# A stream-encoder step on one core: the attention's v made first, its filler moved to the loop's end, the norms' squares summed on 32-column tiles

## The chip, the cores and the metric

The kernel runs on 1 core of one Trainium2 chip. The metric is the device time of one execution in microseconds (us), lower is better. Three timed executions of the kernel before gave 3475.59, 3475.68 and 3482.91 us, median 3475.68 us.

TensorE (PE in the rows) does matmuls and transposes, VectorE is DVE, ScalarE is ACT, GpSimd is POOL, SyncE (SP) only issues DMAs. Each takes its instructions in program order and waits at semaphores. PEld rows are TensorE's weight loads.

## The reference, cut to what matters

One encoder layer over 1152 frames (1024 of a prompt and 8 running streams of 16 frames), width 1024:

```python
x = x + 0.5 * swiglu_ffn(x, ffn1_norm, ...)
h = rmsnorm(x, mix_norm); proj = h @ w_in
#   mixer A: chunk-band softmax attention, 8 heads x 64   mixer B: gated DeltaNet, 4 heads x 128
x = x + (sigmoid(gA) * (yA @ w_branch_a) + sigmoid(gB) * (yB @ w_branch_b)) @ w_mix_out
x = x + cross_attention(rmsnorm(x), K/V of 256 memory tokens)
x = x + 0.5 * swiglu_ffn(x, ffn2_norm, ...)
y = rmsnorm(x, final_norm)          # rmsnorm: x * rsqrt(mean(x*x) + eps) * g, in float32
```

Everything is float32. The memory tokens have a norm of their own before their K and V are made.

## The kernel before, in words

Activations lie transposed: 8 chunks of 128 features on the partitions, 1152 frames along the free axis, worked on in three thirds of 384 frames. A dense product of one weight unit (128 output features) with one third is `product` (L149): every float32 operand is split into a high and a low part, and 3 x 8 matmuls of 384 columns (high x high, weight high x x low, weight low x x high) add into one PSUM bank. POOL makes the split weights (`w_hi` L124 or L143, `w_lo` L127 or L146) in three slots; SP loads them.

The stages run in this order: `memory` (K and V of the memory tokens, with the first norm done beside it), `ffn1`, `attention` (mixer A), `delta` (mixer B), `merge`, `mix`, `cross`, `wo`, `ffn2`, `last`. Engines meet only by semaphores within a stage.

**The norms** (class `Norm`). For each third n: ACT squares the 8 chunks in two instructions of 4 chunks (`square`, L470); `sums` (L479) on PE multiplies each chunk of squares by a 128x128 matrix of ones, 8 float32 matmuls that add into bank 4+n, so that each partition holds the sum over all features; `root` on ACT (Ln L489, Exp L492) makes the inverse root in `n_rinv`; DVE scales the chunks into `n_tmp` (L509, 8 instructions); ACT rounds them to the high part (`upper`, L519, two instructions), DVE makes the low part (`lower`, L526). There are five norms of x with three thirds each, 15 calls of `sums`, and one call for the memory tokens (256 columns). In `ffn_phase` (both FFNs) the last turn does thirds 0 and 1 of the next norm between its own products: `sums` after the fifth down product of a third, with DVE's scaling woven among its additions. In `residual_phase` (`mix`, `wo`) `sums` follows a product of the order table; ACT then does square, root, upper of third 0 and of third 1 in a row. Third 2 is done in the stage that follows. In `memory` lists by job number (`pe_norm`, `act_norm`) say after which job each step goes; ACT there also rounds weights (L2063), copies K and V out (`m_kv`, `m_nat`) and issues their DMAs, all in one order.

**Attention** works pair by pair of heads, four pairs: pair 0 written out, pairs 1 to 3 as a hardware loop. A pair has 9 dense jobs (q, k, v by three thirds), PE taking them in that order in the loop, and by thirds in pair 0; ACT copies each from PSUM (`take`, L1021; two banks in turn, so that a job waits for the copy of the job two before). Then v is turned: 8 transposes of v (L940), 8 of the streams' v (L943), which ACT copies to `a_vn` (L1036) and `a_vns` (L1039) before the first scores (L831) may start. Nine steps follow: PE computes scores, DVE adds the bias and takes the maximum, ACT exponentiates, DVE normalises, PE turns the probabilities (L876), ACT copies them, PE multiplies them with v (`values`, L901; L888 for the streams). Step 4 is the streams' step: its scores (L838, L844) and values run on 32-column tiles, and step 5 turns the streams' output back (L909). So that PE has work meanwhile, the 12 jobs of mixer B's projections (288 matmuls, L249) are dealt out by a list, the `filler`: two places in each step, before and between the two turns of probabilities, and one place before the last values. Job 20, the last filler job, and job 0 of the next pair use the same PSUM bank; job 0 therefore waits for job 20's copy.

Of the kernel before, what the change touches and what calls it, by code (L numbers as in the profile page):

```python
# [14 lines left out]
D = 1024  # L15
# [56 lines left out]
def load_units(sp, k, first, turns, turn, at_turn=None, then=None):  # L72
# [3 lines left out]
    def one(i, j):  # L76
# [3 lines left out]
        sp.dma_start(k.w_raw[slot(j, turn)][:, :], k.units[turn * i + (first + j)])\  # L80
# [15 lines left out]
    for j in range(k.ahead):  # L96
        users = sharing(j, turn) or [turn - 1]
        sp.wait_ge(k.unit_split.sem, k.unit_split.at(turn * (turns - 1) + users[-1] + 1))
        sp.dma_start(k.w_raw[j][:, :], k.units[first + turns * turn + j]).then_inc(k.raw_landed[j].sem, 16)
# [50 lines left out]
def product(pe, out, tiles, n0, n1):  # L150

    last = len(tiles) - 1
    for part in range(3):
        for i, (wh, wl, xh, xl) in enumerate(tiles):
# [107 lines left out]
def ffn_phase(nc, k, name, norm, x, xh, xl, work, tail, bias_rows=None, memory=None):  # L262
# [24 lines left out]
    def tensor(pe):  # L287
        def turn(i):
            order = order_of(i)
            for g, (u, n) in enumerate(order):  # L290
# [17 lines left out]
                mm = product(pe, k.ps[g % NPS][:, 0:THIRD], tiles, n * THIRD, (n + 1) * THIRD)  # L308
# [7 lines left out]
            for n in range(3):  # L316
                pe.wait_ge(k.h_ready.sem, k.h_ready.at(6 * i + (3 + n + 1)))
                for d in range(KD):
# [11 lines left out]
                    if isinstance(i, int) and i == LAST and n >= 1 and d == 4:  # L330
                        tail.sums(pe, n - 1)

# [7 lines left out]
    def scalar(act):  # L340
# [18 lines left out]
        if norm:  # L359
            norm.square(act, 2)  # L360
            norm.root(act, 2)
# [74 lines left out]
class NormSignals:  # L436
# [3 lines left out]
    def __init__(self, k, name):  # L440
        self.nsq, self.ntotal = k.counter(name + "_squared"), k.counter(name + "_total")
        self.nln, self.nrinv = k.counter(name + "_ln"), k.counter(name + "_rinv")
# [5 lines left out]
class Norm:  # L448
# [24 lines left out]
    def sums(self, pe, n):  # L473

        k, s = self.k, self.s
        for c in range(KD):
            if c % 4 == 0:
                pe.wait_ge(s.nsq.sem, s.nsq.at(2 * n + c // 4 + 1))
            mm = pe.matmul(k.ps[4 + n][:, 0:self.width], k.ones[:, :], self.squares[:, c, self.cols(n)],  # L479
                           start=(c == 0), stop=(c == KD - 1))  # L480
        mm.then_inc(s.ntotal.sem, 1)

    def root(self, act, n):
        k, s = self.k, self.s
        act.wait_ge(s.ntotal.sem, s.ntotal.at(n + 1))
        if n >= 2:
            act.wait_ge(s.nscaled.sem, s.nscaled.at(2 * (n - 1)))
        r = self.rinv[:, n % 2, :]
        act.activation(r, k.ps[4 + n][:, 0:self.width], ACT.Ln, bias=k.eps[:, 0:1], scale=1.0 / D)\  # L489
# [41 lines left out]
    def tensor(self, pe):  # L531
        for n in range(self.nb):
            self.sums(pe, n)

# [8 lines left out]
    def scalar(self, act):  # L543
# [3 lines left out]
        for n in range(self.nb):  # L547
            self.root(act, n)
# [28 lines left out]
def last_norm_phase(nc, k, norm):  # L577
# [11 lines left out]
    def tensor(pe):  # L589
        norm.sums(pe, 2)  # L590

    def scalar(act):
        act.wait_ge(k.x_added.sem, k.x_added.at(NPS))
        norm.square(act, 2)
        norm.root(act, 2)
# [10 lines left out]
class Core:  # L606
# [116 lines left out]

    def counter(self, name, tokens=0):
# [36 lines left out]
def attention_phase(nc, k, norm, decay, xh, xl, x, x_to, work):  # L761
# [31 lines left out]
    filler = Filler(3, 4, [14, 8, 18, 8, 20, 8, 22, 8] + [26, 8] * 5 + [12])  # L793
# [32 lines left out]
    def tensor(pe):  # L826
# [85 lines left out]
        def job(i, g, u, n):  # L912
# [1872 lines left out]
```

## Time and profile before

| | us |
|---|---|
| median of 3 timed executions | 3475.68 |
| the profiled execution, its own time | 3480.32 |
| its span, first to last instruction | 3478.5 |
| PE busy in it | 3293.7 |
| DVE busy | 1288.3 |
| POOL busy | 954.7 |
| ACT busy | 674.7 |

The profile follows one execution of 3480.32 us. The span leaves out 1.8 us at its ends. In the span the mean granted TensorE clock was 0.983 of full speed. The matmul rows give the pipelined duration of each, with an end that is modelled; the cost of a matmul in a row of many is the distance between starts. A float32 matmul that isn't split has two records.

### The profile page before, as it was taken

How to read it: one execution, taken by the hardware profiler on the slowest of the kernel's cores; microseconds unless marked ns; L12 is line 12 of the kernel's file. 1: busy time of each engine (PE TensorE's matmuls, PEld its weight loads, DVE VectorE, ACT ScalarE, POOL GpSimd, SP SyncE). 2: the span in 40 equal slices, each digit the busy share in tenths (PEclk: the TensorE clock that was granted, in tenths of full speed). 3: DMA queues.
4: the chain of work that ended last, by engine and by line, in shares of the span. 5: the costliest groups of instructions: out<-in, count | busy, mean ns of one | idle time of the engine just before them, and what ended most of it. 6: DMA issues, size and time to landing. Idle time of an engine off the chain costs nothing. (4 is left out here: it accounts for less than half of the span.)

```text
span 3478.5 us, 50346 instructions
## 1 busy us (share of the span) xinstructions
PE 3293.7 (95%) x19945; PEld 3129.6 (90%) x19945; DVE 1288.3 (37%) x2289; ACT 674.7 (19%) x1302; POOL 954.7 (27%) x436
## 2 busy tenths in 40 slices
PE   6999999999999999988988979999799999999998
PEld 5999999999889888877887879988599999999997
DVE  3232333332445545642442454232225323233324
ACT  5100000000132422433333332123311000000001
POOL 3433333333313123101001023221123333333331
PEclk9999999999999999989999999999899999999999
DMA  5411111111232133112112144024401111111111
GB/s 181 141 37 48 42 42 42 42 36 43 83 109 107 77 119 117 60 69 80 71 38 93 45 157 156 21 96 156 147 31 43 43 48 40 42 40 41 36 48 55
DMA packets 96556, 254.24 MB, mean 73 GB/s; under 512 B 11552, under 2 KB 52640, under 8 KB 93728
## 3 DMA queue, kind: packets, MB, share of 16 engines
q1 hardware_dynamic: 45568, 146.95, 12.3%
q10 hardware_dynamic: 50848, 105.25, 8.4%
q8 instruction: 109, 1.79, 0.2%
q14 instruction: 31, 0.25, 0.0%
HBM read 199.83 MB, written 52.33 MB: 72 GB/s over the span
## 5 line engine op out<-in xcount | busy, mean ns | idle before, releaser
L124 POOL TENSOR_TENSOR w_hi<-w_raw,zero 128x1024 fp32r<-128x1024 f32 x201 | 385.4, 1917 | 2231.3 <-PE psum L155 1320.0
L155 PE MATMUL psum<-x_hi,w_hi 128*128 128x384 f32 x3024 | 598.2, 338 | 51.5 <-DVE x_lo L2136 32.2
L155 PE MATMUL psum<-x_lo,w_hi 128*128 128x384 f32 x3024 | 592.4, 335 | 0.0
L155 PE MATMUL psum<-x_hi,w_lo 128*128 128x384 f32 x3024 | 589.5, 334 | 0.0
L155 PEld LDWEIGHTS psum<-x_hi,w_hi 128*128 128x128 f32 x3024 | 533.6, 189 | 58.1 <-issue 47.6
L155 PEld LDWEIGHTS psum<-x_lo,w_hi 128*128 128x128 f32 x3024 | 533.9, 189 | 0.0
L155 PEld LDWEIGHTS psum<-x_hi,w_lo 128*128 128x128 f32 x3024 | 530.8, 188 | 0.0
L127 POOL TENSOR_TENSOR w_lo<-w_raw,w_hi 128x1024 fp32r<-128x1024 f32 x201 | 500.0, 2488 | 15.8
L394 DVE TENSOR_TENSOR f_hid<-psum,f_gate 128x384 f32<-128x384 f32 x132 | 73.6, 558 | 861.8 <-PE psum L155 859.3
L349 ACT ACTIVATE f_gate<-psum 128x384 f32<-128x384 f32 x132 | 64.7, 493 | 1477.4 <-PE psum L155 1477.4
L155 PE MATMUL psum<-f_h_hi,w_hi 128*128 128x384 f32 x1056 | 269.1, 335 | 0.0
L155 PE MATMUL psum<-f_h_hi,w_lo 128*128 128x384 f32 x1056 | 267.9, 334 | 0.0
L155 PE MATMUL psum<-f_h_lo,w_hi 128*128 128x384 f32 x1056 | 267.9, 334 | 0.0
L249 PE MATMUL psum<-x_hi,w_hi 128*128 128x384 f32 x912 | 197.1, 346 | 3.2 <-issue 2.6
L249 PE MATMUL psum<-x_hi,w_lo 128*128 128x384 f32 x912 | 199.5, 346 | 0.0
L249 PE MATMUL psum<-x_lo,w_hi 128*128 128x384 f32 x912 | 197.8, 346 | 0.0
L155 PEld LDWEIGHTS psum<-f_h_hi,w_hi 128*128 128x128 f32 x1056 | 190.7, 188 | 1.1
L155 PEld LDWEIGHTS psum<-f_h_hi,w_lo 128*128 128x128 f32 x1056 | 190.7, 188 | 0.0
L155 PEld LDWEIGHTS psum<-f_h_lo,w_hi 128*128 128x128 f32 x1056 | 190.7, 188 | 0.0
L406 DVE SCALAR_TENSOR_TENSOR x_late<-psum,x_late 128x384 f32<-128x384 f32 x264 | 145.2, 556 | 116.6 <-PE psum L155 116.6
L406 DVE SCALAR_TENSOR_TENSOR x_early<-psum,x_early 128x384 f32<-128x384 f32 x264 | 145.1, 556 | 112.7 <-PE psum L155 112.7
L249 PEld LDWEIGHTS psum<-x_hi,w_hi 128*128 128x128 f32 x912 | 157.4, 188 | 10.0 <-issue 6.9
(276 smaller groups left out, 3354.2 us busy)
## 6 DMA issues: line engine op xcount, KB each, us to landing
w_raw<-units SPq DMA_DIRECT2D x224, 512.0 KB, 3.5
gate_dram<-b_stash ACTq DMA_DIRECT2D x48, 192.0 KB, 1.9
e_gate<-gate_dram ACTq DMA_DIRECT2D x48, 192.0 KB, 2.5
a_kc<-k_cache ACTq DMA_DIRECT2D x4, 2048.0 KB, 7.5
a_vc<-v_cache ACTq DMA_DIRECT2D x4, 2048.0 KB, 13.9
x_sk<-mem_k ACTq DMA_DIRECT2D x8, 1024.0 KB, 8.5
proj_dram<-a_cv ACTq DMA_DIRECT2D x12, 576.0 KB, 2.8
b_pad<-proj_dram SPq DMA_DIRECT2D x12, 576.0 KB, 4.8
```

The source lines that it names most:

```text
L124: pool.tensor_tensor(k.w_hi[s][:, :], k.w_raw[s][:, :], k.zero[:, 0:1].to_broadcast([P, D]), ALU.add)\
L127: pool.tensor_tensor(k.w_lo[s][:, :], k.w_raw[s][:, :], k.w_hi[s][:, :].bitcast(F32), ALU.subtract).then_inc(k.unit_split.sem, 1)
L155: mm = pe.matmul(out, wl if part == 2 else wh, (xl if part == 1 else xh)[:, n0:n1], start=(part == 0 and i == 0), stop=(part == 2 and i == ...
L249: mm = pe.matmul(k.ps[g % 2][:, 0:THIRD], w[:, c * P:(c + 1) * P], (xl if part == 1 else xh)[:, c, n * THIRD:(n + 1) * THIRD], start=(r == 0),
L349: act.activation(gate[:, n, :], k.ps[g % NPS][:, 0:THIRD], ACT.Silu)\
L394: dve.tensor_tensor(hid[:, j % 2, :], up, gate[:, n, :], ALU.mult).then_inc(k.hid_made.sem, 1)
L406: dve.scalar_tensor_tensor(out=xs, in0=k.ps[g % NPS][:, 0:THIRD], scalar=0.5, in1=xs, op0=ALU.mult, op1=ALU.add).then_inc(k.x_added.sem, 1)
```

## The change

Three things are changed.

1. `Norm.sums`: the chunk c goes to column tile c % 4 (stationary operand 128x32 ones, output on 32 partitions at 32 * (c % 4)); chunks 0 to 3 start the four accumulations, chunks 4 to 7 end them. Bank 4+n then holds four partial sums, each on 32 partitions. A new `gather` on ACT copies them to `n_rinv`, and a new `total` on PE (one float32 matmul of 384 columns with the full ones) adds over all 128 partitions; every value is counted 32 times, and the Ln's scale becomes 1/(32 * D). `total` is placed one step behind `sums`: inside the next product, behind its first 8 of 24 matmuls (`between`), in the FFNs' last turn after the next down product, in `memory` two jobs later, and at once in the last norm and in the memory tokens' norm.
2. Attention: the units of a pair are loaded and made in the order v, q, k. In the loop v is turned (`turn_v`) after the sixth job, and ACT copies it (`copy_v`) after its sixth take; in pair 0 `turn_v` comes after all nine jobs. The pair's first scores wait for seven copies, step 3 for all nine.
3. The filler's list: step 4, and steps 6 to 8, give 23 instead of 26 matmuls at their first place, step 5 30; the place before the last values gives 6 instead of 12, and a new place behind the last values 14.

```diff
+def product(pe, out, tiles, n0, n1, between=None):
     for part in range(3):
+        if part == 1 and between:
+            between()
...
-            mm = pe.matmul(k.ps[4 + n][:, 0:self.width], k.ones[:, :], self.squares[:, c, self.cols(n)],
-                           start=(c == 0), stop=(c == KD - 1))
-        mm.then_inc(s.ntotal.sem, 1)
+            r = 32 * (c % 4)
+            mm = pe.matmul(k.ps[4 + n][r:r + 32, 0:self.width], k.ones[:, 0:32], self.squares[:, c, self.cols(n)],
+                           start=(c < 4), stop=(c >= 4), tile_position=(0, r))
+        mm.then_inc(s.nparts.sem, 1)
+    def total(self, pe, n):
+        pe.wait_ge(s.ngathered.sem, s.ngathered.at(n + 1))
+        pe.matmul(k.ps[4 + n][:, 0:self.width], k.ones[:, :], self.rinv[:, n % 2, :], start=True, stop=True)\
+            .then_inc(s.ntotal.sem, 1)
+    def gather(self, act, n):
+        act.wait_ge(s.nparts.sem, s.nparts.at(n + 1))
+        if n >= 2:
+            act.wait_ge(s.nscaled.sem, s.nscaled.at(2 * (n - 1)))
+        act.activation(self.rinv[:, n % 2, :], k.ps[4 + n][:, 0:self.width], ACT.Copy).then_inc(s.ngathered.sem, 1)
...
+    def nth_unit(self, phase, j):
+        return (2, 0, 1)[j] if phase == 2 and j < 3 else j
-    filler = Filler(3, 4, [14, 8, 18, 8, 20, 8, 22, 8] + [26, 8] * 5 + [12])
+    filler = Filler(3, 4, [14, 8, 18, 8, 20, 8, 22, 8] + [23, 8] + [30, 8] + [23, 8] * 3 + [6, 14])
...
         def pair(i):
-            pe.wait_ge(k.evacuated.sem, k.evacuated.at(DONE * i + (9 + ND)))
...                                         # the 16 transposes go to turn_v(i)
+            pe.wait_ge(k.evacuated.sem, k.evacuated.at(DONE * i + (7 + ND)))
             pe.wait_ge(k.vn_ready.sem, k.vn_ready.at(2 * i + 2))
             for s in range(STEPS):
+                if s == 3:
+                    pe.wait_ge(k.evacuated.sem, k.evacuated.at(DONE * i + (9 + ND)))
...
             filler.products(k, pe, i, 2 * STEPS, xh, xl)
             values(i, STEPS - 1)
+            filler.products(k, pe, i, 2 * STEPS + 1, xh, xl)
...
         with pe.Fori(1, PAIRS) as i:
             for g in range(9):
                 job(i, g, g // 3, g % 3)
+                if g == 5:
+                    turn_v(i)
...
                 take(i, g, g // 3, g % 3)
                 if g == 5:
+                    copy_v(i)
                     load_caches(i)
...
             for g in filler.finished(2 * STEPS):
                 evacuate(i, g)
             copy_o(STEPS - 1)
+            for g in filler.finished(2 * STEPS + 1):
+                evacuate(i, g)
```

Three places where PE's order shows it. First, PE in the last turn of ffn1, around the first `sums`; of before (`f_h` is the FFN's hidden vector):

```order
L155 MATMUL psum<-f_h_hi,w_lo_62 128x384
L479 MATMUL psum<-n_squares,ones 128x384 x8
L155 MATMUL psum<-f_h_hi,w_hi_58 128x384
L155 MATMUL psum<-f_h_hi,w_hi_59 128x384
L155 MATMUL psum<-f_h_lo,w_hi_58 128x384
```

and of the changed kernel:

```order
L157 MATMUL psum<-f_h_hi,w_lo_62 128x384
L489 MATMUL psum<-n_squares,ones 32x384 x8
L157 MATMUL psum<-f_h_hi,w_hi_58 128x384
L157 MATMUL psum<-f_h_hi,w_hi_59 128x384
L157 MATMUL psum<-f_h_lo,w_hi_58 128x384
L157 MATMUL psum<-f_h_lo,w_hi_59 128x384
L157 MATMUL psum<-f_h_hi,w_lo_61 128x384
L157 MATMUL psum<-f_h_hi,w_lo_62 128x384
L497 MATMUL psum<-n_rinv,ones 128x384
```

The eight full matmuls became eight of 32 output rows, and one full matmul follows a product (six matmuls) later. Second, PE in the loop from the last job to the first scores of a pair, before:

```order
L155 MATMUL psum<-x_lo,w_hi_59 128x384 x8
L155 MATMUL psum<-x_hi,w_lo_62 128x384 x8
L938 REGISTER_ALU
L940 MATMUL psum<-ident,a_v 128x128 x8
L943 MATMUL psum<-ident,a_v 16x128 x8
L945 ISA
L831 MATMUL psum<-a_k,a_q 128x128 x2
```

and now:

```order
L157 MATMUL psum<-x_lo,w_hi_59 128x384 x8
L157 MATMUL psum<-x_hi,w_lo_62 128x384 x8
L947 REGISTER_ALU
L157 MATMUL psum<-x_hi,w_hi_59 128x384 x8
L157 MATMUL psum<-x_lo,w_hi_59 128x384 x8
L157 MATMUL psum<-x_hi,w_lo_62 128x384 x8
L980 ISA
L862 MATMUL psum<-a_k,a_q 128x128 x2
```

The transposes stand three jobs earlier and nothing is between the last job and the scores. Third, PE at the end of the loop's body, before:

```order
L876 MATMUL psum<-ident,a_sc 128x128 x5
L249 MATMUL psum<-x_lo,w_hi_58 128x384 x4
L249 MATMUL psum<-x_hi,w_lo_61 128x384 x8
L882 REGISTER_ALU
L897 REGISTER_ALU
L901 MATMUL psum<-a_pt,a_vn 64x128 x10
L962 REGISTER_ALU
L962 COMPARE_AND_BRANCH
```

and now:

```order
L907 MATMUL psum<-ident,a_sc 128x128 x5
L251 MATMUL psum<-x_hi,w_hi_58 128x384 x4
L251 MATMUL psum<-x_lo,w_hi_58 128x384 x2
L913 REGISTER_ALU
L928 REGISTER_ALU
L932 MATMUL psum<-a_pt,a_vn 64x128 x10
L251 MATMUL psum<-x_lo,w_hi_58 128x384 x6
L251 MATMUL psum<-x_hi,w_lo_61 128x384 x8
L1001 REGISTER_ALU
L1001 COMPARE_AND_BRANCH
```

Six matmuls stand before the last values where 12 stood, and 14 between them and the branch.

## Rows read from the trace of the kernel before

**Rows 1.** The page's first part: busy us (share) xinstructions

```profile
PE 3293.7 (95%) x19945; PEld 3129.6 (90%) x19945; DVE 1288.3 (37%) x2289; ACT 674.7 (19%) x1302; POOL 954.7 (27%) x436
```

**Rows 2.** Groups by shape: names, shapes, xcount | busy us, mean ns | idle before

```profile
L479 PE MATMUL psum<-n_squares,ones 128*128 128x384 f32 x240 | 80.1, 487 | 3.1 <-ACT n_squares L470 3.1
L2370 PE MATMUL psum<-x_sk,x_qz 128*32 128x256 f32 x128 | 18.4, 382 | 0.0
```

**Rows 3.** The chain that ended last, stage wo: start, us, what

```profile
2602.85 5.16 PE psum L479 x16
...
2612.26 1.99 POOL w_hi L143
```

**Rows 4.** Timeline of PE, streams' step: start, us, engine, line, names, [idle before]

```profile
1164.98 1.06 PE L838 MATMUL psum<-a_kc,a_qbd 128*32 128x512 f32 x8
1165.87 0.23 PE L844 MATMUL psum<-a_k,a_qbd 128*32 128x16 f32 x8
```

**Rows 5.** Timeline: one float32 matmul of 384 columns; ACT's copy of 384 columns

```profile
1627.85 0.81 PE L1655 MATMUL psum<-b_sq,ones 128*128 128x384 f32 x2
...
982.73 0.49 ACT L1021 ACTIVATE a_q<-psum 128x384 f32<-128x384 f32 x1 [7.84 <-PE psum L155]
```

**Rows 6.** Timeline of ACT, stage mix, the squares of third 1

```profile
2242.54 2.86 ACT L470 ACTIVATE n_squares<-x_late 128x1536 f32<-128x1536 f32 x2 [2.78 <-DVE x_late L2306]
```

**Rows 7.** Timeline of PE, first turn of ffn2, the third 2

```profile
2641.67 1.63 PE L155 MATMUL psum<-x_hi,w_hi 128*128 128x384 f32 x8 [0.78 <-DVE x_lo L526]
```

**Rows 8.** Timeline of ACT and PE, end of ffn1

```profile
937.55 1.49 ACT L519 ACTIVATE x_hi<-n_tmp 128x1536 fp32r<-128x1536 f32 x1 [1.49 <-DVE n_tmp L509]
...
949.30 2.72 PE L155 MATMUL psum<-x_hi,b_w8h 128*8 128x384 f32 x8 [4.62 <-DVE b_w8l L1373]
```

**Rows 9.** Timeline of the end of the kernel

```profile
3459.90 2.86 ACT L470 ACTIVATE n_squares<-x_late 128x1536 f32<-128x1536 f32 x2 [2.58 <-DVE x_late L406]
3461.44 5.43 PE L479 MATMUL psum<-n_squares,ones 128*128 128x384 f32 x16 [2.17 <-ACT n_squares L470]
3466.90 0.58 ACT L489 ACTIVATE n_rinv<-psum,eps 128x384 f32<-128x384 f32 x1 [4.14 <-PE psum L479]
```

**Rows 10.** Timeline of stage memory, ACT and PE

```profile
15.71 0.47 ACT L489 ACTIVATE nm_rinv<-psum,eps 128x256 f32<-128x256 f32 x1 [4.52 <-PE psum L479]
...
86.89 2.08 PE L155 MATMUL psum<-mem_hi,w_hi 128*128 128x256 f32 x8 [2.37 <-POOL w_lo L2029]
```

**Rows 11.** Timeline of PE, last matmuls of pair 1's jobs to its first scores

```profile
1133.61 1.55 PE L155 MATMUL psum<-x_hi,w_lo 128*128 128x384 f32 x8
1135.74 1.09 PE L940 MATMUL psum<-ident,a_v 128*128 128x128 f32 x8 [0.58 <-ACT a_v L1021]
...
1138.84 0.49 PE L831 MATMUL psum<-a_k,a_q 64*128 64x128 f32 x4 [1.13 <-ACT a_vns L1039]
```

**Rows 12.** Timeline of pair 0's start, DVE and PE

```profile
1012.84 0.11 DVE L1168 MEMSET a_bias<- 64x64 f32 x1 [2.10 <-DMA a_bias_s<-bias_dram]
...
1017.02 0.33 PE L876 MATMUL psum<-ident,a_sc 128*128 128x128 f32 x1 [1.26 <-DVE a_sc L1198]
```

**Rows 13.** Timeline of PE at the loop's turn, pair 1 to 2 and 2 to 3

```profile
1220.99 1.31 PE L901 MATMUL psum<-a_pt,a_vn 128*64 128x128 f32 x20
1225.33 2.87 PE L155 MATMUL psum<-x_hi,w_hi 128*128 128x384 f32 x8 [3.02 <-issue]
1227.99 1.94 PE L155 MATMUL psum<-x_lo,w_hi 128*128 128x384 f32 x8
...
1354.63 2.53 PE L155 MATMUL psum<-x_hi,w_hi 128*128 128x384 f32 x8 [2.89 <-issue]
```

**Rows 14.** Busy time by window, PE alone: window, us, PE busy, granted clock, DMA share, GB/s

```profile
1225.00:1229.00 4.00, 3.67 (x12) 0.57 0.88 268
```

**Rows 15.** Timeline of PE from pair 0 into the loop

```profile
1097.42 1.68 PE L155 MATMUL psum<-x_hi,w_hi 128*128 128x384 f32 x8
```

**Rows 16.** Timeline of PE, pair 1, step 5

```profile
1185.09 0.77 PE L876 MATMUL psum<-ident,a_sc 128*128 128x128 f32 x5 [0.89 <-DVE a_sc L1198]
```

More of the change, by code:

```diff
@@ L79, in one @@
             sp.wait_ge(k.unit_split.sem, k.unit_split.at(turn * i + (last + 1 - turn * back)))
-        sp.dma_start(k.w_raw[slot(j, turn)][:, :], k.units[turn * i + (first + j)])\
+        sp.dma_start(k.w_raw[slot(j, turn)][:, :], k.units[turn * i + (first + k.nth_unit(k.phase, j))])\
             .then_inc(k.raw_landed[slot(j, turn)].sem, 16)
@@ L98, in load_units @@
         sp.wait_ge(k.unit_split.sem, k.unit_split.at(turn * (turns - 1) + users[-1] + 1))
-        sp.dma_start(k.w_raw[j][:, :], k.units[first + turns * turn + j]).then_inc(k.raw_landed[j].sem, 16)
+        sp.dma_start(k.w_raw[j][:, :], k.units[first + turns * turn + k.nth_unit(k.phase + 1, j)]).then_inc(k.raw_landed[j].sem, 16)
 def units_ahead(k):
@@ L307, in turn @@
                           xh[:, c, :], xl[:, c, :]) for c in range(KD)]
-                mm = product(pe, k.ps[g % NPS][:, 0:THIRD], tiles, n * THIRD, (n + 1) * THIRD)
+                mm = product(pe, k.ps[g % NPS][:, 0:THIRD], tiles, n * THIRD, (n + 1) * THIRD,
+                             (lambda: norm.total(pe, 2)) if order is by_third and g == 2 else None)
                 mm.then_inc(k.dense_done.sem, 1)
@@ L331, in turn @@
                         tail.sums(pe, n - 1)
+                    if isinstance(i, int) and i == LAST and n >= 1 and d == 5:
+                        tail.total(pe, n - 1)
         if memory:
@@ L360, in scalar @@
             norm.square(act, 2)
+            norm.gather(act, 2)
             norm.root(act, 2)
@@ L375, in scalar @@
         tail.square(act, 0)
+        tail.gather(act, 0)
         tail.root(act, 0)
@@ L380, in scalar @@
             tail.upper(act, 0)
+        tail.gather(act, 1)
         tail.root(act, 1)
@@ L590, in tensor @@
         norm.sums(pe, 2)
+        norm.total(pe, 2)
     def scalar(act):
@@ L594, in scalar @@
         norm.square(act, 2)
+        norm.gather(act, 2)
         norm.root(act, 2)
@@ L910, in turn_streams, with job @@
             mm.then_inc(k.ys_turned.sem, 1)
-        def job(i, g, u, n):
+        def job(i, g, u, n, between=None):
             if n == 0:
@@ L930, in first_jobs @@
                 for u in range(3):
-                    job(0, 3 * n + u, u, n)
+                    job(0, 3 * n + u, u, n, (lambda: norm.total(pe, 2)) if n == 0 and u == 1 else None)
                     if n == 0 and u == 0:
@@ L1109, in scalar @@
         take(0, 0, 0, 0)
+        norm.gather(act, 2)
         norm.root(act, 2)
@@ L2272, in tensor @@
                      for c in range(KD)]
-            product(pe, k.ps[j % NPS][:, 0:THIRD], tiles, n * THIRD, (n + 1) * THIRD).then_inc(k.dense_done.sem, 1)
+            product(pe, k.ps[j % NPS][:, 0:THIRD], tiles, n * THIRD, (n + 1) * THIRD,
+                    (lambda: tail.total(pe, SUMMED[j - 1])) if j - 1 in SUMMED else None).then_inc(k.dense_done.sem, 1)
             if j in SUMMED:
@@ L2290, in scalar @@
             tail.square(act, n)
+            tail.gather(act, n)
             tail.root(act, n)
@@ L2419, in tensor @@
                      for c in range(KD)]
-            product(pe, k.ps[g % 2][:, 0:THIRD], tiles, n * THIRD, (n + 1) * THIRD).then_inc(k.dense_done.sem, 1)
+            product(pe, k.ps[g % 2][:, 0:THIRD], tiles, n * THIRD, (n + 1) * THIRD,
+                    (lambda: norm.total(pe, 2)) if g == 2 else None).then_inc(k.dense_done.sem, 1)
             if g == 1:
@@ L2458, in scalar @@
         evacuate(0, 1, 0)
+        norm.gather(act, 2)
         norm.root(act, 2)
```

47 lines of the change are left out of this document (28 added, 19 removed).

## The prediction, on record before the changed kernel ran

> **What bounds the kernel.** First the page's busy times: PE is busy for 95% of the span, no other engine for over 37% [rows 1]. So an edit pays where it takes work from PE or an idle gap out of PE's row, as far as nothing else is late behind it. Then the groups by shape, for the price of PE's work; then the chain that ended last and the timeline around each of the 16 norm sums and the four pairs, for who releases PE there. The chain runs through PE's products and sums, and once per residual stage through POOL, which begins to split the last weights when a product of PE ends [rows 3]; a gain on PE ahead of that moves POOL too. In the stage of the memory tokens ACT's order is the bound, since PE waits for POOL, and POOL for ACT's rounding [rows 10].
>
> **Part 1, the sums: price of one call.** 240 records of 128x384 keep PE busy 80.1 us [rows 2]: 15 calls of 5.3 us, and 5.16 us each on the chain [rows 3]. The nearest row to what replaces them is the streams' scores: four float32 matmuls of 512 columns on four 32-column tiles (8 records) take 0.89 us from their first start to the next group's [rows 4], where four full ones one after the other would take four times that. For 384 columns this is 0.67 us for four, 1.33 for the two rounds. I add 0.3 for going to narrow tiles and back, an estimate of about one pipeline tail each way (0.17 us is what a row of matmuls shows beyond its last start). `total` is one full float32 matmul, 0.81 less that tail, 0.64 us [rows 5]. New price 2.3, saving 2.9 us a call. Bounds: were the tiles to pass as slowly as the cross attention's streams, 0.144 us a record of 256 columns (18.4/128, [rows 2]), the rounds would take 3.5 us and the saving be 0.8; without any overlap the call would lose 0.9. On the upper side, with no cost of switching, 3.2. I take 2.9, since the operands, the type and the rotation over four tiles are those of rows 4, while in the slower row four matmuls in succession stay on one tile.
>
> The Trainium skill, "TensorE: Matmul & The Clock Gate", section "Measured speedup vs the span model", gives 3.07 for four tiles instead of the full factor. By it the rounds would take 5.16/3.07, an estimate of 1.7 us, and each call would save 0.4 us less. The row above shows nearly the full factor here.
>
> **Part 1, what gets through.** The new chain behind the sums is: ACT sees the end, copies 384 columns (0.49 us, [rows 5]), PE adds. With the semaphores some 0.8 us; the piece of product put between takes 1.4 us (8 matmuls, 1.55 less the tail, [rows 11]) or 1.04 in the FFNs, so where ACT is free PE doesn't wait. The inverse root comes about 1.3 to 1.7 us sooner, not 2.9.
> - Memory tokens, four calls. The first is on the way to everything: its root starts at 15.7 [rows 10], now some 1.4 us sooner. The other three leave PE sooner, but ACT sits in `upper` waiting for DVE (2.3 us at 54.1, rows 10) and PE later waits for POOL (2.37, same rows). Moving the root behind the next job takes away ACT's idling between, and keeps the units' rounding ahead. I walked ACT, PE and POOL through jobs 4 to 15 with the rows' durations and get 3 to 5 us; I take 4.5 with the first call, bounds 0 and 8.
> - End of ffn1: two calls, 5.8 on PE. But `gather` of third 1 stands behind `upper` of third 0 on ACT, whose second half waits for DVE's scaling [rows 8], which goes at the pace of the products. `total` then waits some 1.5 us. Net 4.3. PE's wait of 4.62 us for DVE that follows [rows 8] moves along, since DVE starts it behind PE's last product.
> - Third 2 in attention: the second half of the squares comes 1.4 us after the first, so round two waits; 2.3.
> - mix and wo: third 0 saves 2.9. Third 1 comes too soon for its squares: they begin behind DVE's low part and addition [rows 6], which follow the root and gain only 1.3; PE waits 1.4. Net 4.4 to 4.7, I take 4.6 each. Third 2: PE would save 2.9, but its product of third 2 waits for DVE already [rows 7], and that chain gains 1.7 with the root. 1.7 each. Together 12.6.
> - End of ffn2: no `upper` stands in between, so 5.8. The last call is bare: sums 5.43, with squares until 3462.8 and the root at 3466.9 [rows 9]. New: second round to 3463.5, copy to 3464.2, total to 3465.1, root at 3465.2: 1.7. Together 7.5.
>
> Sum of part 1: 4.5 + 4.3 + 2.3 + 12.6 + 7.5 = 31.2 us.
>
> **Part 2, v first.** In pairs 1 to 3 PE idles 0.58 before the transposes, for the copy of v, and 1.13 before the scores, for `a_vns` [rows 11]. Both go: the transposes follow a job with v long copied, ACT's two copies lie beside three jobs of 4.2 us, and the seven copies that the scores need are done. What is late next is DVE's first normalised row, which had slack; ACT issues two DMAs before its first exponential, at most 0.5 us. 3 x 1.7 = 5.1. In pair 0 nothing: the wait before the first scores shrinks, but DVE begins when the bias has landed (at 1012.8), and PE waits for DVE at 1017.0 anyway [rows 12]. The cache loads are issued 3 us later and are wanted 25 us on.
>
> **Part 3, the filler.** At both turns of the loop PE has only the last values (20 records, 1.31 us) queued when it reaches the branch and idles 3.02 and 2.89 us [rows 13]; the granted clock is 0.57 over the next 4 us [rows 14], so partly at 1.2 instead of 2.4 GHz, and the first 16 matmuls take 2.87 + 1.94 where 1.68 + 1.55 is usual [rows 13, 15], 1.6 us more. Fourteen matmuls at 0.173 (1.04/6, or 1.55 less the tail over 8) are 2.4 us of work under this gap. But job 20, which shares a bank with job 0, now ends there, and its copy (tail, semaphores, 0.49) comes first: at least 0.8 us idle; with the branch reached a little later I take 1.0. The clock then stays up. 2 x (2.0 + 1.6) = 7.2. Against it: between pair 0 and the loop there was no idle at all [rows 15], now 0.8 for that copy; and behind pair 3 the copy and its store are issued 0.8 later, in front of the stores that end the phase. The first places give 3 fewer at steps 4 and 6 to 8, 4 more at step 5, where PE waits 0.89 us for DVE [rows 16]: that wait shrinks by 0.7 and step 6's grows by 0.5, since DVE's chain fixes both; +0.1. Sum: 7.2 - 0.8 - 0.8 + 0.1 = 5.7.
>
> **The sum.** 31.2 + 5.1 + 5.7 = 42.0 us. Against the profiled execution's own time, 3480.3 (span 3478.5 and 1.8 around it), that gives 3438.3. The median of the timed runs lies 4.6 us under that execution; from it, 3475.7 - 42.0 = 3433.7, and I predict 3434.
>
> **Rivals.**
> - The tiles overlap partly, as in the slower of rows 2. 15 calls save 2.1 less, about 27 us in all after what was lost to waits anyway: 3461. For it: that row. Against it: rows 4. By the skill's factor (named above) it would be 5 us less gain, inside my range. 0.07.
> - The filler doesn't cover the turn: PE's waits and the copy of job 20 leave a gap of 2 to 3 us and the clock still falls. 7 us less: 3441, and with pair 0's end also slower 3443. For it: two new waits; against: the 14 matmuls wait for nothing. 0.12.
> - The waits for `gather` bite everywhere, because ACT is later than I read: 1.5 us at each of 12 further places: 3452. For it: ACT's order in the last turn of ffn1; against: ACT idles 4 to 7 us before its roots, as 4.14 in rows 9. 0.07.
> - Slower: column tiles run one after the other when each tile's sum has two matmuls open in one bank. Then a call costs 5.16 + 0.3 + 0.64, 0.9 more than now, and with the copy on the way of each root some 1.8 more on the six chains that go through it; 15 x 0.9 + 6 x 1.8 is 24 us lost against 10.8 won: 3489. It decides from a call price of about 5.9 us. For it: only that accumulation on narrow tiles is timed nowhere alone. 0.02.
>
> **How the numbers follow.** The forecast's case, 0.72, spans 3424 to 3446: the memory stage's bounds (0 to 8), the switching cost (0 to 0.6 a call) and the loop's turns (2 to 9). The range 3424 to 3453 takes in the second and third rival. The difference that a measurement can tell from none is about 0.2%, 7 us. Every case but the last lies beyond it: faster 0.97, same 0.01, slower 0.02.
>
> **What would show it.** The 15 groups of squares' records take 1.5 to 1.8 us from start to the next product, `total` 0.64 inside the next product without idle before it, except at the end of ffn1 (1.5). PE's idle before the pair's first scores is gone; at the loop's turn it is about 1 us and the granted clock stays at 1. Squares of third 1 in mix and wo have PE waiting about 1.4. Wrong if the narrow matmuls start more than 0.2 us apart, if PE still idles over 2 us at the turns, or if the span falls less than 25 us.

## The result, and the profile after

Five timed executions of each kernel on one chip: before 3479.18 us (3475.59 to 3482.91), after 3455.45 us (3452.68 to 3461.32), ratio 0.9931, 95% interval 0.9917 to 0.9945. Faster, as forecast, but by 24 us and not by 42; the predicted 3434 us and the range up to 3453 were missed. A second series of six executions of the same changed kernel gave 0.9938 (0.9921 to 0.9955). The profiled execution of the changed kernel took 3452.68 us, its span is 27.6 us shorter than before's.

The page's first part, to be held against [rows 1]: PE has 42 us less to do, and the span is 27.6 us shorter. PE's idle time, the span less the busy time, grew from 184.8 to 199.5 us.

```profile
PE 3251.4 (94%) x19977; PEld 3088.2 (89%) x19977; DVE 1283.0 (37%) x2289; ACT 680.9 (20%) x1318; POOL 948.7 (27%) x436
```

Where both profiles stand, by the start of the same PE instruction in each (first product of ffn1 107.53 and 105.62, first sums of ffn1's end 922.75 and 918.29, first product behind it 949.30 and 940.03, first squares of mixer B 1496.53 and 1480.49, first sums of mix 2227.39 and 2207.99, wo's first product 2503.48 and 2480.63, first sums of the kernel's end 3437.34 and 3416.60, end of the span):

| stretch | forecast gain | measured |
|---|---|---|
| memory tokens | 4.5 | 1.9 |
| ffn1 up to its last turn | 0 | 2.6 |
| end of ffn1 | 4.3 | 4.8 |
| attention (2.3 + 5.1 + 5.7) | 13.1 | 6.8 |
| mixer B, merge | 0 | 3.4 |
| mix and cross attention | 6.3 | 3.4 |
| wo, ffn2 up to its last turn | 6.3 | -2.1 |
| end of ffn2, last norm | 7.5 | 6.9 |
| sum (rounded) | 42.0 | 27.6 |

**The price of a call was right.** The groups by shape that answer to [rows 2], and the timeline of PE at third 0 in wo (start, us, names, idle before):

```profile
L489 PE MATMUL psum<-n_squares,ones 128*32 128x384 f32 x240 | 27.3, 564 | 12.6 <-ACT n_squares L479 12.6
L497 PE MATMUL psum<-n_rinv,ones 128*128 128x384 f32 x30 | 13.3, 526 | 3.8 <-ACT n_rinv L506 3.8
```

```profile
2562.33 1.50 PE L489 MATMUL psum<-n_squares,ones 128*32 128x384 f32 x16
2563.76 1.66 PE L157 MATMUL psum<-x_hi,w_hi 128*128 128x384 f32 x8
2565.25 0.81 PE L497 MATMUL psum<-n_rinv,ones 128*128 128x384 f32 x2
2565.60 1.85 PE L157 MATMUL psum<-x_lo,w_hi 128*128 128x384 f32 x8
2567.29 1.55 PE L157 MATMUL psum<-x_hi,w_lo 128*128 128x384 f32 x8
```

From the first of the matmuls over the squares to the third part of the product are 4.96 us; two parts of a product take 2.77 (2 x 8 starts 0.173 apart), so sums and `total` cost 2.19 us, where 2.3 was forecast and 5.16 were paid before [rows 3]. The sums alone take 1.43, 3.6 times less than before. By the speedup of 3.07 that the Trainium skill has for four tiles ("TensorE: Matmul & The Clock Gate", "Measured speedup vs the span model") they would take an estimated 1.7; the trace stands nearer to the full factor of four. The page's 3.07 is of four row tiles, a direction in which nothing is split here; it has no row of four column tiles. But PE now waits 12.6 us for squares where it waited 3.1 [rows 2]. For third 1 in mix and wo it waits 0.8 each, where 1.4 was forecast.

**Where it was lost: wo.** The timelines of DVE, POOL, ACT and PE behind `sums` of third 1, first of before, then of after:

```profile
2609.22 8.09 DVE L509 SCALAR_TENSOR_TENSOR n_tmp<-x_late,gains,n_rinv 128x384 f32<-128x384 f32 x8 [5.78 <-ACT n_rinv L492]
2625.00 2.86 ACT L470 ACTIVATE n_squares<-x_late 128x1536 f32<-128x1536 f32 x2 [6.17 <-DVE x_late L2306]
2627.24 5.32 PE L479 MATMUL psum<-n_squares,ones 128*128 128x384 f32 x16
```

```profile
2583.12 11.85 DVE L532 SCALAR_TENSOR_TENSOR n_tmp<-x_late,gains,n_rinv 128x384 f32<-128x384 f32 x8 [5.37 <-ACT n_rinv L515]
2594.90 0.54 DVE L2358 TENSOR_TENSOR x_late<-x_late,psum 128x384 f32<-128x384 f32 x1
...
2584.77 2.31 POOL L143 TENSOR_TENSOR w_hi<-w_raw,zero 128x1024 fp32r<-128x1024 f32 x1 [34.56 <-PE psum L157]
2587.16 2.56 POOL L146 TENSOR_TENSOR w_lo<-w_raw,w_hi 128x1024 fp32r<-128x1024 f32 x1
2589.69 2.21 POOL L124 TENSOR_TENSOR w_hi<-w_raw,zero 128x1024 fp32r<-128x1024 f32 x1
2591.97 2.59 POOL L127 TENSOR_TENSOR w_lo<-w_raw,w_hi 128x1024 fp32r<-128x1024 f32 x1
2594.52 2.21 POOL L124 TENSOR_TENSOR w_hi<-w_raw,zero 128x1024 fp32r<-128x1024 f32 x1
...
2602.67 2.86 ACT L479 ACTIVATE n_squares<-x_late 128x1536 f32<-128x1536 f32 x2 [6.17 <-DVE x_late L2358]
...
2604.21 2.88 PE L489 MATMUL psum<-n_squares,ones 128*32 128x384 f32 x16 [5.14 <-ACT n_squares L479]
```

DVE's eight scalings of third 1 take 8.09 us before and 11.85 after (4.33 where POOL is silent). Counted from the first sums of wo (2585.05 and 2562.33), the scalings of third 1 began 3.4 us sooner than before, and POOL, whose slot is freed by one of PE's products, 4.8 us sooner: 1.65 us behind DVE's first scaling, where it was 3.04 before (2612.26, [rows 3]). Two scalings fewer got through ahead of it: before, six of 0.61 us (0.53 from start to start), then 2.25 and 2.73; after, four of 0.61, then 2.25, 2.72, 2.24 and 2.74. Each of these last four ends 0.4 us behind one of POOL's first four instructions. All behind it is late: the squares of third 2, for which PE waits 5.14 us. The clock falls: windows of after (PE, PEld, DVE, ACT, POOL busy; granted clock; DMA share; GB/s):

```profile
1212.00:1216.00 4.00, 3.87 (x22) 3.88 (x23) 0.00 (x0) 0.00 (x0) 3.92 (x3) 1.00 0.83 297
2604.00:2609.00 5.00, 4.79 (x22) 2.39 (x23) 0.00 (x0) 2.02 (x3) 0.00 (x0) 0.51 0.00 0
2619.00:2623.00 4.00, 3.71 (x13) 3.74 (x14) 3.22 (x7) 0.52 (x2) 0.00 (x0) 0.57 0.00 0
```

The second and third stand at 1.2 of 2.4 GHz for most of their length, each behind a wait of PE (5.14, then 2.17 for third 2's low part); the sums there take 2.88 instead of 1.50.

**A pair's start and its steps.** Timelines of DVE, POOL and PE of after, pair 1:

```profile
1127.80 2.08 DVE L1246 TENSOR_SCALAR a_sc<-a_sc,a_rinv 128x128 f32<-128x128 f32 x1
1129.81 0.15 DVE L1244 RECIPROCAL a_rinv<-a_rsum 128x1 f32<-128x1 f32 x1
1129.99 0.29 DVE L1246 TENSOR_SCALAR a_sc<-a_sc,a_rinv 128x128 f32<-128x128 f32 x1
...
1125.48 1.89 POOL L124 TENSOR_TENSOR w_hi<-w_raw,zero 128x1024 fp32r<-128x1024 f32 x1 [9.78 <-PE psum L157]
1127.45 2.36 POOL L127 TENSOR_TENSOR w_lo<-w_raw,w_hi 128x1024 fp32r<-128x1024 f32 x1
...
1129.94 0.33 PE L907 MATMUL psum<-ident,a_sc 128*128 128x128 f32 x1 [1.47 <-DVE a_sc L1246]
...
1184.02 0.77 PE L907 MATMUL psum<-ident,a_sc 128*128 128x128 f32 x5 [1.77 <-DVE a_sc L1246]
...
1212.13 1.66 PE L157 MATMUL psum<-x_hi,w_hi 128*128 128x384 f32 x8 [0.96 <-ACT a_stash L1020]
1213.63 1.55 PE L157 MATMUL psum<-x_lo,w_hi 128*128 128x384 f32 x8
```

Both idles of [rows 11] are gone, but one normalisation of 128 columns takes 2.08 us, ending with POOL's split, where the next one takes 0.29. PE waits 1.47 us for it, in all three pairs of the loop. At the loop's turn 3.02 [rows 13] became 0.96, and the next parts take 1.66 and 1.55 where they took 2.87 and 1.94: as forecast. At step 6 stands a wait of 1.77; before it was 0.89 at step 5 [rows 16] and 0.24 at step 6. Behind pair 3 the first squares of mixer B come late, before and after:

```profile
1496.53 2.93 PE L1535 MATMUL psum<-b_sq,ones 128*128 128x384 f32 x4 [14.51 <-ACT b_sq L1693]
```

```profile
1480.49 2.93 PE L1583 MATMUL psum<-b_sq,ones 128*128 128x384 f32 x4 [16.55 <-ACT b_sq L1741]
```

**The kernel's end.** ACT's root starts at 3439.28 of 3450.9 us, and 3466.90 of 3478.5 before [rows 9]:

```profile
3434.84 2.88 PE L489 MATMUL psum<-n_squares,ones 128*32 128x384 f32 x16 [2.17 <-ACT n_squares L479]
3438.33 0.91 PE L497 MATMUL psum<-n_rinv,ones 128*128 128x384 f32 x2 [0.61 <-ACT n_rinv L506]
...
3439.28 0.58 ACT L512 ACTIVATE n_rinv<-psum,eps 128x384 f32<-128x384 f32 x1 [1.00 <-PE psum L497]
```

### The profile page after: what moved, and what is told of

Same layout as the page of the kernel before. It is cut to its first block and busy times, and to the rows that moved or that the text cites. A ratio compares the mean times of both kernels' runs of the same rounds, so it can differ in the third digit from the quotient of the medians.

```text
span 3450.9 us, 50434 instructions
## 1 busy us (share of the span) xinstructions
PE 3251.4 (94%) x19977; PEld 3088.2 (89%) x19977; DVE 1283.0 (37%) x2289; ACT 680.9 (20%) x1318; POOL 948.7 (27%) x436
```

## The experiments

Theory P, formed from the rows above: POOL's weight splitting stretches DVE instructions that read and write SBUF alone (not all of them, see the last section), and each part of the change brings DVE's work nearer to a split. Ratios are against the kernel before on the same chip, with 95% intervals; places are compared by the profiles.

There is one profile per kernel, so a difference between two profiles is held against what profiles with the same code in a place differ by. In the five with the changed kernel's attention (the changed kernel twice, e6, e7 and e8 below) that stage takes 540.5 to 542.8 us up to the first squares of mixer B: nearly all of it in pair 0, 145.9 to 148.5 us. Pair 2 takes 125.8 to 126.0 in them.

**Each part alone (e1_sums, e2_v_first, e3_filler).** The edits are parts 1, 2 and 3 of the diff, each put on the kernel before.

> Part 1 alone: the kernel before with the sums on 32-column tiles, gather and total; units in the old order, the old filler list. Theory P (POOL's weight splitting stretches DVE's SBUF instructions, and the sums' saving brings the two together in the stages mix and wo): a call costs 2.2 us instead of 5.16, DVE's 8 scalings of third 1 take 11.9 us in mix and in wo instead of 8.1, PE waits about 5 us for the squares of third 2 in wo, and of the 31 us forecast for this part 20 to 24 arrive: time near 0.9935 of before. Rival R (part 1 brings its 31 us where nothing else is changed, and what the whole kernel lacks was lost by the edits in attention, which shift everything behind them): 0.991, scalings at 8 us.

> Part 2 alone: v made and turned first, all else as before. Theory P: PE's idle 0.58 + 1.13 before the transposes and the first scores of pairs 1 to 3 goes, but DVE's first normalisation (0.29 us alone) now falls into POOL's splitting of the unit that the last job freed, takes about 2.1 us, and PE waits 1.5 us for it: 3 x 0.2, no difference that can be measured. Rival R (the forecast): 3 x 1.7 = 5.1 us faster, 0.9985, no wait before the first transpose of probabilities.

> Part 3 alone: the new filler list, all else as before. Both theories: PE's wait at the two loop turns goes from 3.0 and 2.9 to about 1 us and the granted clock stays up there, 7.3 us won. Theory P: given back are 2 us behind pair 3, where the last filler job now ends with PE's last matmul and its copy and store are late, 0.6 before the loop, and 0.6 per pair at steps 5 and 6: 2.3 us net, 0.9993. Rival R (the forecast): 0.8 + 0.8 given back and +0.1 at the steps: 5.7 us net, 0.9984.

| | ratio | end of attention, gain, us | start of the kernel's last sums, gain, us |
|---|---|---|---|
| sums | 0.9938 (0.9925 to 0.9951) | 11.9 | 26.5 |
| v first | 0.9994 (0.9985 to 1.0002) | 3.6 | 3.6 |
| filler | 0.9990 (0.9979 to 1.0002) | 5.7, of which 2.6 before attention | 10.7 |
| all (changed kernel) | 0.9931 (0.9917 to 0.9945) | 16.0 | 26.6 |

The sums bring nearly all of the measured gain; neither of the others can be told from nothing. In e1_sums the scalings of third 1 take 11.85 us in mix and in wo, so the loss there belongs to part 1 itself: P and not R. In e2_v_first every pair of the loop has the wait of 1.47 us at its start. Beyond the 0.2 per pair it won 1.0 in pair 0, which neither theory had (the 0.84 us wait for v's copy in front of the transposes is gone there too), and the clock did not fall at one of the two turns, though PE waited 2.77 there. e3_filler won the turns (0.96 and 0.58 us), and has the waits of 1.62 to 1.78 at step 6, the 0.58 in front of the loop and 16.21 behind pair 3. The 10.7 of its one profile can't be laid to the edit: its timed executions lie between 3464.7 and 3485.3 us. Nor do the timed executions of v first show its 3.6.

**POOL held at a pair's start (e4_hold_pair).**

```diff
+        def hold(i, j):
+            if j == 5:
+                pool.wait_ge(k.normed.sem, k.normed.at(2 * STEPS * i + 2))
```

`hold` is called in front of each unit's split.

> The changed kernel; POOL holds the split of unit 5 of a pair (the unit that the pair's last dense job frees) until DVE has normalised the pair's first two rows. Theory P: DVE's first normalisation is back at 0.29 us, PE's 1.47 us wait at the start of pairs 1 to 3 is gone, 4.4 us faster than the changed kernel, since unit 5 is wanted 25 us later: 0.992 of before. Rival R (DVE's instruction is late for another reason, such as ACT's two DMA issues ahead of its first exponential, or its own reading of a place that PE or a DMA uses): the 2.1 us and the wait stay, and nothing is won.

0.9922 (0.9910 to 0.9935). DVE and POOL, pair 1:

```profile
1128.93 0.28 DVE L1252 TENSOR_SCALAR a_sc<-a_sc,a_rinv 128x128 f32<-128x128 f32 x1
1129.33 0.29 DVE L1252 TENSOR_SCALAR a_sc<-a_sc,a_rinv 128x128 f32<-128x128 f32 x1
...
1129.70 1.89 POOL L126 TENSOR_TENSOR w_hi<-w_raw,zero 128x1024 fp32r<-128x1024 f32 x1 [12.83 <-DVE a_sc L1252]
```

The normalisation is back at 0.28, PE's wait is gone from all three pairs, pair 2 takes 124.1 us instead of 125.8, and attention is 4.3 us shorter than in the changed kernel. P holds, R falls: ACT's two DMA issues are still there. By the timed runs alone e4 can't be told from the changed kernel (0.9931, 0.9917 to 0.9945).

**POOL held in mix and wo (e6_hold_both, e7_hold_second).** POOL waits for `nscaled` of third 1, in front of the next stage's first unit (e6), or of its second only (e7):

```diff
-        split_units(pool, k, 1, used_after(order, 1))
+        split_units(pool, k, 1, used_after(order, 1),
+                    hold_ahead=lambda: pool.wait_ge(tail.s.nscaled.sem, tail.s.nscaled.at(4)))
```

> The changed kernel; in mix and wo POOL splits the first unit of the next stage (and with it the second, which is behind it) only when DVE has scaled third 1. Theory P: DVE's 8 scalings of third 1 take 4.3 us in both stages instead of 11.9; PE waits some 3 us for the first unit's low part instead of 0.9 to 1.1, the second comes in time; the squares of third 2 begin some 7 us earlier, the 5.14 us wait in wo is gone, and with it the low clock (1.4 + 1.6 us). Net 3 to 5 us over both stages. Rival D (DVE is slow in this stretch because of PE's or DMA's traffic, not POOL's): the scalings still take over 8 us, and the kernel is 2 to 5 us slower than the changed one.

> As e6_hold_both, but the first unit is split at once and only the second one waits for the scaling. Theory P: the scalings overlap one unit's split instead of two, 8.1 us instead of 11.9; PE waits 0.9 for the first unit as now and some 2 for the second; the wait for the squares of third 2 falls from 5.14 to under 1, and the clock stays: 3 to 5 us faster than the changed kernel. Rival D: scalings unchanged, 2 us slower per stage.

DVE's scalings in wo, with the first unit held, and with the second held; behind each the PE instruction that waits longest:

```profile
2588.45 4.32 DVE L536 SCALAR_TENSOR_TENSOR n_tmp<-x_late,gains,n_rinv 128x384 f32<-128x384 f32 x8 [5.34 <-ACT n_rinv L519]
...
2592.94 1.90 POOL L147 TENSOR_TENSOR w_hi<-w_raw,zero 128x1024 fp32r<-128x1024 f32 x1 [37.38 <-DVE n_tmp L536]
...
2598.70 1.65 PE L161 MATMUL psum<-x_hi,w_hi 128*128 128x384 f32 x4 [4.52 <-POOL w_lo L150]
2609.69 1.50 PE L493 MATMUL psum<-n_squares,ones 128*32 128x384 f32 x16
```

```profile
2587.23 8.08 DVE L537 SCALAR_TENSOR_TENSOR n_tmp<-x_late,gains,n_rinv 128x384 f32<-128x384 f32 x8 [5.37 <-ACT n_rinv L520]
...
2593.89 1.66 PE L161 MATMUL psum<-x_hi,w_hi 128*128 128x384 f32 x8 [0.93 <-POOL w_lo L150]
2601.24 2.74 PE L161 MATMUL psum<-x_hi,w_hi 128*128 128x384 f32 x8 [2.91 <-POOL w_lo L129]
2607.16 1.50 PE L494 MATMUL psum<-n_squares,ones 128*32 128x384 f32 x16
```

4.32, 8.08, 11.85 us with none, one and two units beside the scaling: the three values that P gave. The 5.14 us wait is gone in both. From wo's first sums to ffn2's last turn e6 is 3.6 us and e7 4.9 us shorter than the changed kernel (850.6 and 849.3 us; the seven profiles without a hold there have 854.2 to 854.4, and e1_sums 852.1). Over mix and cross nothing is shown: e6 is 0.8 longer and e7 1.0 shorter, but profiles in which nothing is edited there differ by 2 us. e6 pays with 4.52 for the first unit, 1.5 more than expected. And the low clock, which was to go with the wait, moved: behind the waits of 4.52 and 2.91 the next eight matmuls take 2.93 and 2.74 us where 1.66 is usual (granted clock 0.50 from 2598 to 2602 in e6). Timed: 0.9924 (0.9910 to 0.9938) and 0.9909 (0.9893 to 0.9925), both of which overlap the changed kernel's interval. With PE and DMA unchanged in kind and POOL alone moved, D is out.

**Steps 5 to 7 (e5_hold_two, e9_hold_step7, e10_list).** In e5 and e9 POOL holds unit 0 of the next pair as well, until DVE's rows of step 6 or of step 7:

```diff
+            if j == 0 and not isinstance(i, int):
+                pool.wait_ge(k.normed.sem, k.normed.at(2 * STEPS * i - 4))     # e9: - 2
```

```diff
-    filler = Filler(3, 4, [14, 8, 18, 8, 20, 8, 22, 8] + [23, 8] + [30, 8] + [23, 8] * 3 + [6, 14])
+    filler = Filler(3, 4, [14, 8, 18, 8, 20, 8, 22, 8] + [26, 8] * 3 + [22, 8] * 2 + [6, 14])     # e10
```

> The changed kernel with the hold of unit 5 (as in the run e4_hold_pair), and in addition POOL splits unit 0 of the next pair only after DVE's two rows of step 6, in pairs 0 to 2. Theory P (POOL's splits at step 5 stretch DVE's chain of steps 5 and 6, and PE waits 1.77 us for its end): the copy of 1.87 us and the product of 2.82 us between the two steps fall to 0.2 to 1 us, the wait at step 6 goes in pairs 0 to 2, and stays at 1.77 in pair 3: 3 x 1.7 = 5 us faster than e4_hold_pair. Rival F (the wait comes from the new list, 23 matmuls at step 6 instead of 26, and not from POOL): it stays at 1.5 or more in all pairs.

> As e5_hold_two, but unit 0 of the next pair is split only after DVE's two rows of step 7, where DVE has nothing to do for 4.7 us and POOL needs 4.3. Theory P: in pairs 0 to 2 no convolution or normalisation of DVE overlaps that split; PE's wait of 1.77 us at step 6 is gone as in e5_hold_two, and the 1.98 us at step 7 that took its place there is gone too: 3 x 1.7 = 5 us faster than e4_hold_pair in attention. Rival W (unit 0 then comes too late for the next pair's first job): PE waits 1 us or more for POOL at each loop turn, and nothing is won.

> The changed kernel with another list: 26 matmuls at the first place of steps 4, 5 and 6, 22 at steps 7 and 8, and 6 and 14 at the end as in the change. Theory N (the list only decides whether PE or DVE reaches the end of DVE's chain first, and 23 at step 6 is 3 too few): waits at steps 5 and 6 as before the change, 0.9 and 0.2 instead of 1.77, unless steps 7 or 8 now wait; about 0.6 us a pair, 2.5 us. Rival S: the same time is waited elsewhere, the sum of PE's waits in a pair stays at 1.8 and nothing is won.

From a pair's first product to the next pair's, in us (pair 2): before 129.3, changed kernel 125.8, e4 124.1, e5 124.7, e9 122.3, e10 126.2. e5 lost the wait at step 6 and found one of 1.98 at step 7, where the held split now met the convolution: the collision had moved, and the expected 5 us did not come. In e9 PE waits for DVE no more in pairs 1 and 2; attention is 4.6 us shorter than in e4. In both, PE's wait of 1.77 at step 6 stays in pair 3, where nothing is held: with the same list in all pairs, F falls. W falls too: at the loop's turns PE waits for ACT's copy (0.91 and 0.58), not for POOL. POOL in e9, in the stretch in which DVE has nothing:

```profile
1194.51 1.89 POOL L126 TENSOR_TENSOR w_hi<-w_raw,zero 128x1024 fp32r<-128x1024 f32 x1 [19.73 <-DVE a_sc L1256]
1196.48 2.35 POOL L129 TENSOR_TENSOR w_lo<-w_raw,w_hi 128x1024 fp32r<-128x1024 f32 x1
...
1199.16 0.82 DVE L1240 TENSOR_TENSOR a_sc<-psum,a_bias 128x640 f32<-128x640 f32 x1 [4.73 <-PE psum L872]
```

Timed: e5 0.9926 (0.9912 to 0.9941), e9 0.9904 (0.9890 to 0.9918), the one hold that stands clear of the changed kernel timed in its own series (0.9938, 0.9921 to 0.9955). The other list (e10, 0.9947, 0.9933 to 0.9960) turned 1.77 into 0.88 and 0.27 and won nothing: with DVE's chain stretched, matmuls moved between steps 4 and 8 only change where PE waits.

**The memory stage (e8_memory).**

```diff
-    pe_norm = {3: [sums 0], 5: [total 0, sums 1], 7: [total 1, sums 2], 9: [total 2]}
+    pe_norm = {3: [sums 0], 4: [total 0], 5: [sums 1], 6: [total 1], 7: [sums 2], 8: [total 2]}
```

(names shortened), and ACT's gather, root and upper one job earlier each.

> The changed kernel with other lists in the stage of the memory tokens: ACT's gather one job earlier (behind jobs 3, 5 and 7), total behind the next job instead of the second next, root and upper where they were before the change (4, 6, 8). Theory A (ACT's order bounds the stage; the root one job later costs 2.9 us on ACT, because ACT waits for the next job's bank and its DMA first): first root of x at about 49 instead of 53.6 us, the first product of ffn1 2 to 4 us earlier. Rival M (the stage is bound by POOL's low parts and by the weight loads): first product of ffn1 within 0.5 us of the changed kernel's 105.6.

0.9934 (0.9920 to 0.9948), no difference to the changed kernel. The first root of x starts at 47.4 instead of 53.6, the first product of ffn1 at 104.2 instead of 105.6, and in other profiles of unchanged memory stages that product starts anywhere from 104.5 to 106.7. Theory A fell, with 1.4 us for its 2 to 4: the root's place is not what holds the stage. M's mark, within 0.5 of 105.6, was missed too, but no further than the scatter goes. In the first 105.6 us PE is busy 69.1 us where it was 77.1 in 107.5. Of these 8 us, 6 came back as waits: those for ACT's copy of a job's result grew from 3.5 to 7.5 us and 2.9 for its gathers are new, while those for POOL's low parts fell from 15.6 to 14.6. What holds ACT there stays open.

**The same kernel again, and all together (a1_after_again, e11_best).** e11 has the holds of e4, e7 and e9, the lists of e8, and in ffn1:

```diff
-        if bias_rows:
-            act.wait_ge(k.unit_split.sem, k.unit_split.at(3))
-            bias_rows.store(act)
+                if bias_rows and isinstance(i, int) and i == 0 and c == 0:
+                    bias_rows.store(act)      # behind the first three gates; DVE's spread likewise
```

> The changed kernel once more, nothing edited: what two profiled executions of one kernel differ by, place by place. Theory L (part of what the first two profiles differ by is not the change's: in ffn1's first turn the bias table lands 9.1 or 11.7 us after its issue, and PE waits 0 or 2.3 us; the stages of mixer B took between 726.3 and 731.6 us in ten profiles, whatever the edit): places before attention's end as in the first profile within 0.5 us apart from that one wait, mixer B's stages up to 3 us off. Rival C (the 2.5 us in ffn1 and 3.3 us in mixer B are the change's): both come again as in the first profile.

> All that helped, together: the changed kernel with POOL held at a pair's start (e4_hold_pair), at step 7 (e9_hold_step7) and for the second unit behind mix and wo (e7_hold_second), the memory stage's lists of e8_memory, and in ffn1's first turn the bias rows' spreading and store moved behind the first three gates. If the parts add up as the places of their profiles say (4.0 + 5 + 6.0 + 1.4, and 2.3 in the executions where the table lands late): 16 to 18 us faster than the changed kernel, 0.988 of before. If they take from each other as v first and the filler did: 0.990.

Of the 13 profiles in which ffn1's first turn is as it was, six have this wait of before, and seven, the two of the changed kernel among them, have none or at most 0.28:

```profile
127.02 1.68 PE L155 MATMUL psum<-x_hi,w_hi 128*128 128x384 f32 x8 [2.32 <-ACT f_gate L349]
```

It is the same collision as in wo. ACT's gates stand behind its store of the bias rows, and that behind DVE's copy in SBUF, which starts when the bias table has landed: by the profiles, 6.6 to 7.2 us after its issue in the seven, 7.9 to 9.3 in the six. (The 9.1 and 11.7 of the expectation are the distances to the issue of the store, and take in the copy.) POOL and DVE, before and after:

```profile
120.62 1.89 POOL L124 TENSOR_TENSOR w_hi<-w_raw,zero 128x1024 fp32r<-128x1024 f32 x1 [4.64 <-PE psum L155]
121.28 3.38 DVE L749 COPY bias_rows<-bias_rows 128x4088 f32<-128x4088 f32 x1 [36.65 <-DMA bias_rows<-table]
```

```profile
117.81 2.29 DVE L780 COPY bias_rows<-bias_rows 128x4088 f32<-128x4088 f32 x1 [30.36 <-DMA bias_rows<-table]
118.67 3.17 POOL L124 TENSOR_TENSOR w_hi<-w_raw,zero 128x1024 fp32r<-128x1024 f32 x1 [3.70 <-PE psum L157]
```

In all seven the copy starts 0.3 to 0.9 us ahead of POOL's high part and takes 2.29; in all six POOL is ahead, and the copy takes 3.05 to 3.70, or, in e9, starts only as POOL's high part ends. A shift of about 1 us decides over 2.3. Kernels with either code fall on either side (e3 has none of the wait, e6, e7 and e9 have it), so it isn't the change's; a1 alone, which has no wait again, would not have told L from C here.

Mixer B is edited nowhere. From its first squares to mix's first sums the 14 profiles took 726.3 to 734.6 us: 730.9 before, 727.5 and 729.3 in the two of the changed kernel, 726.3 in e3, 734.6 in e10. So L holds, though a1 differed by up to 0.9 us ahead of that too: 2.6 in the table above is not the change's, and 3.4 can't be laid to it. Without both the profile's 27.6 become 21.6, near the 23.7 of the timed medians.

e11_best: 3437.09 us (3434.19 to 3440.79), 0.9873 (0.9859 to 0.9887), the fastest: its median is 20.3 us under the changed kernel's in the same series (3457.40), where 16 to 18 were expected, with a span of 3439.0 us and POOL's busy time as in the changed kernel (950.0 for 948.7). In the profile 11.5 us are won up to mixer B, where the parts give some 10, and 3.4 of e7's 4.9 from wo's first sums on: most of the parts add up.

```profile
PE 3252.4 (95%) x19977; PEld 3092.4 (90%) x19977; DVE 1263.2 (37%) x2289; ACT 681.5 (20%) x1318; POOL 950.0 (28%) x436
```

DVE does the same 2289 instructions in 19.8 us less than in the changed kernel. That the 2.3 us in ffn1 are gone by the edit, one profile can't show, since half of the others lack them without it.

## Why the prediction was wrong

- **Price of a call, end of ffn1, kernel's end, third 2 in attention: right.** 2.19 for 2.3; 4.8 for 4.3, with `total` waiting 0.78 where 1.5 was read; 6.9 for 7.5; third 2 in attention 2.7 for 2.3 in e1_sums, by one profile of a stretch that differs by as much between profiles of one code.
- **Third 2 in mix and wo: the step that failed most.** "That chain gains 1.7 with the root" took DVE's scaling and lowering as lengths that move along. They are not: in wo the scaling grew by 3.8 us, because PE's part of the gain ran ahead of the root's (by third 1, 4.8 us at POOL's split and 3.4 at DVE's scaling) and brought the split 1.4 us nearer to it. wo and ffn2 gave -2.1 for 6.3, mix and cross 3.4 for 6.3; with POOL held the stretch of 11.85 is 4.32. The section on what bounds the kernel says that a gain on PE moves POOL too; the sum then did not ask what POOL would meet.
- **v first: mis-sized by its last sentence.** The two idles went as worked out. "What is late next is DVE's first normalised row, which had slack": the slack was that POOL's split of the unit just freed was over by then. 1.47 of 1.7 came back in each pair, which makes 0.7 of the 5.1. Pair 0 gave 1.0 where nothing was forecast.
- **Filler: the turns right, the rest not.** 3.66 and 3.89 were won at the two turns for 3.6 each. Behind pair 3 mixer B's first squares wait 2.0 longer, for which 0.8 was put (ACT's copy and stores of the last job begin only after PE's last matmul), and the steps lost 0.6 a pair where +0.1 in all was put, since DVE's chain there carries POOL's splits too. In front of the loop 0.6 was lost for 0.8.
- **Memory tokens: mis-sized,** 1.9 for 4.5, and 1.6 of it is the first call. "Moving the root behind the next job takes away ACT's idling between" was a walk through the jobs: the first root of x came 3.0 us later (53.60 for 50.63), and PE waits 4.0 us more for ACT's copies. That the root's place was the reason has been tested and is not so; which step of ACT is, stays open.
- **The rivals.** None of the four was what happened. "The waits for `gather` bite everywhere" named the right amount (3452) for a wrong reason: PE waits 3.8 us for gather in all. The likeliest rival lacked was a DVE instruction that is longer when it is moved.

## What to carry to other kernels

Before a wait is taken out or an engine made faster, list what else the ending instruction releases: here each product of PE releases both ACT's chain to DVE and POOL's splits, and the two engines then meet. A duration read in a trace holds for its neighbours in that trace; where one group shows two means for one shape (0.54 and 1.0 us a scaling on average here), find what stood beside the slow ones before adding it to a sum. A wait for the other engine's last short instruction can be worth more than the idle it costs, if it puts the work into a gap, as e9 did with 4.3 us of POOL in 4.7 of DVE.

## What the runs showed of the hardware

- While POOL runs a 128x1024 add or subtract, two kinds of DVE instruction on SBUF alone wait for its end: those with two SBUF inputs (a 128x384 scaling takes up to 2.7 us instead of 0.61), and a product or a copy with one (128x128 2.08 instead of 0.29; the bias rows' copy up to 3.70 instead of 2.29). Others are untouched: one with an input in PSUM (0.54 at 2594.90, beside POOL's high part of 2594.52), and the maximum over 128 columns, though it reads SBUF alone (0.29 at 1126.19 and at 1126.71, beside POOL's high part of 1125.48). The Trainium skill says why ("GPSIMD Engine Reference", "Key points": GpSimd shares its SBUF interfaces with VectorE, and contends with instructions that have two SBUF inputs or use both ports). The trace agrees for two inputs; that the product and the copy use both ports, and the maximum not, would fit, but no run shows it. The price, some 2 us for each POOL instruction met, is this case's.
- POOL waits for DVE in the same way, so it loses what the DVE instruction lasts: a high part takes 2.31 beside the scalings, 3.17 to 3.74 behind the bias rows' copy, and 1.89 alone (e9's rows); a low part 3.73 beside DVE's lowering (in e6 and e7) and 2.35 alone. Whichever is first goes through.
- Four accumulations of two float32 matmuls each, open in one bank on four 32-column tiles, run beside one another: 8 matmuls of 384 columns in 1.43 us.
